# Retention stage of a two-layer hybrid attention block (fp32): rounds of one unit with decay on v, roots and affine products for two units at a time, and the gate in place

## What is computed

```python
log_gamma = jnp.log1p(-jnp.exp2(-5.0 - jnp.arange(h)))
decay = jnp.where(rel[None] >= 0, jnp.exp(jnp.maximum(rel, 0.0)[None] * log_gamma[:, None, None]), 0.0)
xi = jnp.exp((pos[:, None] + 1.0) * log_gamma[None, :])
zeta = jnp.exp((c - 1.0 - pos)[:, None] * log_gamma[None, :])
chunk_decay = jnp.exp(c * log_gamma)
inner = jnp.einsum('bnihd,bnjhd->bnhij', qc, kc) * decay
inner = jnp.einsum('bnhij,bnjhe->bnihe', inner, vc)
new_state = einsum('bjhd,bjhe->bhde', k_i * zeta, v_i) + chunk_decay * state
cross = jnp.einsum('bnihd,nbhde->bnihe', qc, prev_states) * xi
o = inner + cross
o = (o - mu) * lax.rsqrt(var + RET_GN_EPS)      # over the 64 columns of a head
return jax.nn.silu(g) * (o * gn_w + gn_b)
```

## Time and profile before

| | before |
|---|---|
| device time, median of 3 runs | 2778.09 us (2775.32 to 2784.47) |
| the profiled execution's own time | 2785.77 us |
| its span in the profile | 2784.0 us |
| granted TensorE clock, mean | 0.946 of 2.4 GHz |
| PE busy | 2620.7 us (94%) |
| DVE, ACT, POOL busy | 1537.3, 1105.9, 1036.0 us |
| retention stage of layer 0 (first transpose to first product of the output projection) | 558.0 to 653.0 us |
| the same of layer 1 | 1934.3 to 2029.3 us |

### The profile page before, as it was taken

The page is one execution under the profiler, slowest core; times in us unless marked ns, Lnnn a source line. Parts: engine busy times, 40 slices in busy tenths (PEclk is TensorE's granted clock), DMA queues, the critical chain, the costliest instruction groups (busy, mean ns, idle before and its releaser), DMA issues. The chain is left out here.

```text
span 2784.0 us, 43220 instructions
## 1 busy us (share of the span) xinstructions
PE 2620.7 (94%) x13164; PEld 2256.6 (81%) x13164; DVE 1537.3 (55%) x2969; ACT 1105.9 (40%) x2567; POOL 1036.0 (37%) x1229
## 2 busy tenths in 40 slices
PE   6999998989999999999989998988998999999997
PEld 5999877867778888888879998877777888888886
DVE  4666544373465445477656665433726544545785
ACT  4444543262532232244444445433515332323444
POOL 3455522183144544301044554221811555442012
PEclk9999999958999999999999999998599999999999
DMA  5111101121223332483331101012022323335633
GB/s 173 28 34 43 34 10 37 36 85 61 103 72 109 105 109 90 148 295 95 102 107 31 33 19 39 6 37 89 31 90 75 110 80 108 113 102 204 233 97 121
DMA packets 238653, 243.09 MB, mean 87 GB/s; under 512 B 27904, under 2 KB 170752, under 8 KB 238464
## 3 DMA queue, kind: packets, MB, share of 16 engines
q1 hardware_dynamic: 238464, 240.83, 26.9%
HBM read 173.14 MB, written 67.63 MB: 86 GB/s over the span
## 5 line engine op out<-in xcount | busy, mean ns | idle before, releaser
L2281 POOL TENSOR_TENSOR fw_a_lo<-fw_a_raw,fw_a_hi 128x512 fp32r<-128x512 f32 x132 | 179.9, 1363 | 524.1 <-DVE fw_s_raw L1875 524.1
L2281 POOL TENSOR_TENSOR fw_s_lo<-fw_s_raw,fw_s_hi 128x512 fp32r<-128x512 f32 x176 | 229.8, 1318 | 51.9 <-ACT fw_s_hi L1393 51.9
L702 PE MATMUL banks<-ht_hi,da_hi 128*128 128x512 f32 x496 | 192.9, 389 | 0.0
L702 PE MATMUL banks<-ht_lo,da_hi 128*128 128x512 f32 x496 | 192.9, 389 | 0.0
L702 PE MATMUL banks<-ht_hi,da_lo 128*128 128x512 f32 x496 | 192.9, 389 | 0.0
L702 PE MATMUL banks<-w_diff_hi,ht_hi 128*128 128x384 f32 x512 | 182.0, 355 | 6.2 <-DVE ht_lo L1579 4.1
L1206 ACT ACTIVATE pt_hi<-banks 128x512 fp32r<-128x512 f32 (+2 forms) x144 | 67.4, 502 | 291.1 <-PE banks L805 291.0
L702 PE MATMUL banks<-w_diff_hi,ht_lo 128*128 128x384 f32 x512 | 173.6, 339 | 0.0
L702 PE MATMUL banks<-w_diff_lo,ht_hi 128*128 128x384 f32 x512 | 173.5, 339 | 0.0
L2120 POOL TENSOR_TENSOR qk_rot<-rope_a,rope_b 128x512 f32<-128x512 f32 x64 | 82.7, 1292 | 213.5 <-DVE rope_b L1608 213.5
L1636 DVE TENSOR_REDUCE stats<-banks 128x1 f32<-128x1024 f32 (+3 forms) x192 | 138.6, 749 | 40.1 <-PE banks L903 35.3
(11 more groups left out here) (354 smaller groups left out, 7781.5 us busy)
## 6 DMA issues: line engine op xcount, KB each, us to landing
da_raw<-act_scratch SPq DMA_DIRECT2D x154, 256.0 KB, 2.7
fw_a_raw<-in_w_gate_dram SPq DMA_DIRECT2D x88, 256.0 KB, 3.1
act_scratch<-act_s SPq DMA_DIRECT2D x66, 256.0 KB, 2.9
w_diff_raw<-in_w_in_dram SPq DMA_DIRECT2D x24, 512.0 KB, 6.0
fw_a<-in_w_up_dram SPq DMA_DIRECT2D x44, 256.0 KB, 3.2
fw_a_raw<-in_w_up_dram SPq DMA_DIRECT2D x44, 256.0 KB, 2.9
act_scratch<-act_zero SPq DMA_DIRECT2D x44, 256.0 KB, 2.4
act_scratch<-act_one SPq DMA_DIRECT2D x44, 256.0 KB, 2.8
```

The source lines that it names most:

```text
L702: mm = pe.matmul(bank, lhsT, rhs, start=first and i == 0, stop=last and i == len(pairs) - 1, skip_group_check=resumes)
L2281: pool.tensor_tensor(w[1][:], w[2][:], w[0][:].bitcast(F32), ALU.subtract).then_inc(S["f_lo"], 1)
```

## The change

The decay between tokens i and j of a chunk, gamma^(i-j), is taken apart. v of token j is scaled by gamma^-(j+1)/8 (in place, on DVE, during latent attention), the score table becomes a plain causal 0/1 matrix, and the outer factor gamma^(i+1) is left out: the norm over a head's 64 columns cancels it, if the epsilon is divided by its square. So q and k need no scaled copies: `ret_scaled` is gone, PE transposes two blocks of a unit instead of three, and k is split unscaled. The state is multiplied by chunk_decay when it is split (ACT L1330 by its scale, DVE `ret_state_low` L1827 instead of POOL).

Roots are taken for two units in one call (four values). Normalizing moves from DVE to ACT (`ret_normed`, scale and bias, L1339), for which DVE computes the bias of two units (`ret_offset`, L1835). `ret_finish` multiplies and adds over two units in one instruction each. The gate's silu stays in r_z instead of r_gate.

The loops run over `RET_STEPS`, 24 rounds u. In round u each engine takes what others made in the round ahead. The quarters of the first output weights are split in rounds 4, 7, 10 and 13. `load_out(1)` waits for the finish of ten units (r_mx at 5 pairs), because r_z of units 0 to 9, in its place, now holds gates. The transposes of mixed_rows go in another order: the six columns of blocks that don't come from retention for both halves of the rows, then the last two for both.

```diff
-    rt_hi = [sb(f"rt_hi{i}", [P, 3, P], F32R, HT + 12 * KB + 1536 * i) for i in range(3)]
+    rt_hi = [sb(f"rt_hi{i}", [P, 2, P], F32R, HT + (12 + i) * KB) for i in range(3)]
...
+        RET_STEPS = range(RET_UNITS + 8)
+        ROUND_OUT = {4: 0, 7: 1, 10: 2, 13: 3}
# SP
-                arrives(decay[:], decay_dram.rearrange("p (a n) -> p a n", a=RET_PAIRS), "ret_in")
+                arrives(causal[:], causal_dram, "ret_in")
...
-                sp.wait_ge(S["r_xz"], L * PER["r_xz"] + T + 2)
-                sp.wait_ge(S["r_vlo"], L * PER["r_vlo"] + T + 2)
+                sp.wait_ge(S["r_mx"], L * PER["r_mx"] + T // 2 + 1)
                 sp.sem_inc(S["passed"], 1)
-                sp.wait_ge(S["tr_done"], L * PER["tr_done"] + RING - 2 * 2 * KD - RET_UNITS + T + 2)
                 load_out(1)
...
-                    sp.wait_ge(S["tr_done"], L * PER["tr_done"] + RING - NORM2_RINGS - 2 * KD + (half + 1) * KD)
+                    sp.wait_ge(S["tr_done"], L * PER["tr_done"] + RING - NORM2_RINGS - 2 + 2 * half)
# PE
-                    pe.wait_ge(S["r_xz"], L * PER["r_xz"] + n + 1)
+                    pe.wait_ge(S["rope_sum"], L * PER["rope_sum"] + ROPE_RET + n + 1)
...
-                    pe.transpose(bank[:, tokens(2)], r_xzt[n % 3][:, 0:2, :].rearrange("p a d -> p (a d)"), ident[:])\
-                        .then_inc(S["tr_done"], 1)
...
+                for u in RET_STEPS:
+                    if u < RET_UNITS:
+                        ret_transpose(u // T, u % T)
+                    if 0 <= u - 1 < RET_UNITS:
+                        ret_inner((u - 1) // T, (u - 1) % T)
+                    if 0 <= u - 2 < RET_UNITS:
+                        ret_output((u - 2) // T, (u - 2) % T)
...
-                transpose_rows(mixed_rows[:, 0:4, :], "r_mx", T + 4)
-                transpose_rows(mixed_rows[:, 4:8, :], "r_mx", 2 * T)
+                for blocks in (range(KD - 2), range(KD - 2, KD)):
+                    for half in range(2):
+                        if blocks[0]:
+                            pe.wait_ge(S["r_mx"], L * PER["r_mx"] + T // 2 + 2 * half + 2)
+                        transpose_rows(mixed_rows[:, 4 * half:4 * half + 4, :], "mix_in", 16, blocks)
# ACT
+                def ret_normed(n):
+                    m, i = n // 2, n % 2
+                    b = m % 2
+                    act.wait_ge(S["r_nb"], L * PER["r_nb"] + m + 1)
+                    if m >= 2:
+                        act.wait_ge(S["r_mx"], L * PER["r_mx"] + m - 1)
+                    for j in range(2):
+                        st = act.activation(r_norm[b][:, i, 64 * j:64 * j + 64], r_sum[m % 3][:, i, j, :], ACT.Identity,
+                                            bias=r_nb[:, b, 2 * i + j:2 * i + j + 1], scale=r_rs[:, b, 2 * i + j:2 * i + j + 1])
+                    st.then_inc(S["r_on"], 1)
...
+                for u in RET_STEPS:
+                    if u < RET_UNITS:
+                        ret_high(u)
+                        ret_high_k(u)
+                    if u + 2 < RET_UNITS:
+                        ret_gate_and_v(u + 2)
+                    if 0 <= u - 7 < RET_UNITS:
+                        ret_normed(u - 7)
+                    if 0 <= u - 1 < RET_UNITS:
+                        ret_inner(u - 1)
+                    if u in ROUND_OUT:
+                        weights(CH_OUT, [ROUND_OUT[u]])
                 weights(CH_OUT + 1)
# DVE
+                    v = r_z[n][:, 2 * P:3 * P].rearrange("p (j d) -> p j d", j=2)
+                    dve.tensor_tensor(v, v, xz[:, n // T, 0:2].unsqueeze(2).to_broadcast([P, 2, RET_DIM]), ALU.mult)
...
+                for u in RET_STEPS:
+                    if 0 <= u - 3 < RET_UNITS:
+                        ret_take(u - 3)
+                    if u < RET_UNITS:
+                        ret_low(u)
+                    if 0 <= u - 1 < RET_UNITS:
+                        ret_inner(u - 1)
+                    if 0 <= u - 3 < RET_UNITS:
+                        ret_moments(u - 3)
+                    if u >= 6 and u % 2 == 0 and u // 2 - 3 < RET_UNITS // 2:
+                        ret_offset(u // 2 - 3)
+                    if u + 2 < RET_UNITS:
+                        ret_low_v(u + 2)
+                    if 0 <= u - 1 < RET_UNITS:
+                        ret_state_low(u - 1)
# POOL
+                for u in RET_STEPS:
+                    if u < RET_UNITS:
+                        ret_low_k(u)
+                    if 0 <= u - 1 < RET_UNITS:
+                        ret_inner(u - 1)
+                    if u >= 5 and u % 2 == 1 and (u - 5) // 2 < RET_UNITS // 2:
+                        ret_root((u - 5) // 2)
+                    if u >= 9 and u % 2 == 1:
+                        ret_finish((u - 9) // 2)
+                    if u in ROUND_OUT:
+                        weights(CH_OUT, [ROUND_OUT[u]])
                 weights(CH_OUT + 1)
```

More of the change, by code:

```diff
@@ L1367, in _ @@
                         ret_gate_and_v(n)
[L1368 to L1380 removed]
+                for u in RET_STEPS:
[10 more added lines that the diff above has]
+                        weights(CH_OUT, [ROUND_OUT[u]])
                 weights(CH_OUT + 1)
[L1384 to L1385 removed]
+                for blocks in (range(KD - 2), range(KD - 2, KD)):
+                    for half in range(2):
+                        high_rows(half, None, blocks)
                 def gu_high(m, g, names):
@@ L1880, in h_low @@
                         .then_inc(S["h_lo"], 1)
-                for half in range(2):
-                    low_rows(half, None)
+                for blocks in (range(KD - 2), range(KD - 2, KD)):
+                    for half in range(2):
+                        low_rows(half, None, blocks)
                 for q in range(2 * T):
@@ L2248, in ret_root, with ret_finish @@
+                    pool.wait_ge(S["r_ms"], L * PER["r_ms"] + m + 1)
                     inverse_root(r_rs[:, b, :], r_ms[:, b, :]).then_inc(S["r_rstd"], 1)
-                def ret_finish(n):
-                    b, p = n % 2, n // T
-                    pool.wait_ge(S["r_on"], L * PER["r_on"] + n + 1)
+                def ret_finish(m):
+                    b, p = m % 2, 2 * m // T
+                    pool.wait_ge(S["r_on"], L * PER["r_on"] + 2 * m + 2)
                     cols = slice(p * P, (p + 1) * P)
-                    if n == 0:
+                    w, bias = (x[:, cols].unsqueeze(1).to_broadcast([P, 2, P]) for x in (gn_w, gn_b))
+                    if m == 0:
@@ L2263, in _ @@
[L2263 to L2273 removed]
+                    pool.tensor_tensor(r_norm[b][:], r_norm[b][:], w, ALU.mult).then_inc(S["r_gw"], 1)
@@ new lines, in ret_finish @@
+                    pool.wait_ge(S["r_gw"], L * PER["r_gw"] + m + 1)
+                    pool.tensor_tensor(r_norm[b][:], r_norm[b][:], bias, ALU.add).then_inc(S["r_gb"], 1)
+                    pool.wait_ge(S["r_gate"], L * PER["r_gate"] + 2 * m + 2)
+                    pool.wait_ge(S["r_gb"], L * PER["r_gb"] + m + 1)
+                    for i in range(2):
+                        n = 2 * m + i
+                        st = pool.tensor_tensor(mixed_rows[:, n % T, MIX_RET + p * P:MIX_RET + (p + 1) * P], r_norm[b][:, i, :],
+                                                r_z[n][:, 3 * P:4 * P], ALU.mult)
```

182 lines of the change are left out of this document (60 added, 122 removed).

## The result

| | before | after |
|---|---|---|
| device time, median of 20 runs each | 2778.91 us | 2786.60 us |
| ratio of after to before | | 1.0023, 95% interval 1.0017 to 1.0029 |
| the profiled execution's own time | 2785.77 us | 2787.85 us |
| its span | 2784.0 us | 2786.0 us |
| granted clock, mean | 0.946 | 0.946 |

Every engine has less to do, and the kernel is 0.23% slower. By the ratio the change is +6.4 us (0.0023 of 2779; the two medians differ by 7.7), which is under the 0.3% that the prediction called no change. The median, 2786.6, lies in the whole range of 2765 to 2796, but 0.2 above the bound of no change (2786.4, counted from the earlier median of before, 2778.09; that of the 20 runs is 2778.91) and 0.6 above the likeliest case's own range, 2774 to 2786.

A forecast was written before the change was run, and what follows sets the result against it. PE was taken to bound the later retention units, POOL those with a weight quarter, and ACT's and DVE's blocks the end. (0.0 + 1.2) × 2 layers = +2.4 us gave a median of 2780, whole range 2765 to 2796.

The forecast's parts named there:

- Rounds of 4.35: PE's retention rounds: without the third transpose, each falls by 0.22 us from 4.57 to 4.35.
- Start, taken 0: Start of retention, where DVE waits 3.2 us for gn_b: a saving of 0 to 1 us, taken as 0.
- PE ends about 629.1: End of PE's retention units: about 629.1 instead of 639.5, a gain of 10.4 us per layer inside the stage.
- POOL's pair: POOL's work in two rounds: root 1.4, finish 2.5, sum 6.1 us, 8.4 with a quarter, against PE's 8.7.
- SP asks at 630.9: Request for the second output weights: issued at 630.9 after the tenth unit's finish, landing at 638.70.
- The last finishes at 634.4, 636.9 and 639.4: POOL's pairs 5 to 7 at the stage's end: each 2.5 us, finished ahead of the banks.
- The gain is handed back, 0.0: Stage end: late weights in ACT's queue put the projection at 653.0 against 652.98, 0.0 us per layer; chance 0.62.
- The clock in the tail, 0 to +2.7, taken +1.2: Tail transposes of mixed_rows: up to twelve blocks at half clock, 0 to +2.7 us per layer, taken +1.2.
- Rival B, the full clock in the stage: Retention stage at 2.4 GHz: PE's round halves, POOL becomes the bound, about 2759 us; chance 0.07.
- Rival D, DVE and POOL hold each other up: Retention rounds: DVE's small SBUF instructions drawn out beside POOL's, DVE pacing the stage; 2793 us, chance 0.15.
- Rivals C and E: C: fifth finish three to five us earlier, about 2770, chance 0.10. E: tail at half clock, 2783 to 2788, chance 0.06.
- Scaling v costs nothing: Latent attention: DVE's 16 small products hidden under PE, taken 0, at most 9 us if DVE were the bound.

The follow-up runs named there:

- the repeat: The changed kernel run and traced once more, unchanged; 1.0022 of the kernel before, 2786.6 us.
- rows_first: Changed kernel with ACT's blocks of mixed_rows ahead of its copies of the second output weights; 0.9978 of the kernel before, 2774.9 us.
- before_rows_first: Kernel before with ACT's blocks of mixed_rows put ahead of its copies of the second output weights; ratio 0.9992.
- gates_own: Changed kernel with gates of units 0 to 9 in own tiles, so the second output weights are requested early; 1.0010 of the kernel before, 2782.6 us.
- before_dve2: Kernel before with two extra value-preserving DVE products per retention unit during latent attention, ACT's copy of v waiting for DVE; ratio 1.0017.
- no_vscale: Changed kernel without the scaling of v by the decay; 1.0008 of the kernel before.
- best3: Changed kernel with ACT's blocks reordered ahead of weights' copies, three normalized-pair tiles, weight quarters in rounds 1 to 4, v scaled on POOL; ratio 0.9929, 2758.3 us.
- early_quarters: Changed kernel with the four weight quarters in rounds 1 to 4 instead of 4, 7, 10 and 13; 1.0018 of the kernel before, 2783.8 us.

## Why the prediction was right, and where it was not

The path was right and the verdict was right by little: the forecast was +2.4 us and 2780, measured were +6.4 and 2786.6, at the very edge of what was called no change. Two costs that stood at nothing in the sum, the scaling of v and DVE held up by POOL, were not nothing, and a start that came earlier than forecast offset part of them. That the class came out is in part luck.

Of the steps, in the prediction's order, with times from the request for the table (558.3 in the kernel before, 557.2 in after):

- *Rounds of 4.35.* Measured 4.34 to 4.36 from unit 3 on. Two rounds are shorter, 3.7 and 2.97, by 2.0 us together where the prediction subtracted 1.8, and the one with the third quarter takes 4.43 to 4.50, or 6.7 as the long round.
- *Start, taken 0.* This term was off. Unit 3's first transpose stood at +10.3 before, and stands at +7.4 to +8.5 in the four layers of the changed kernel, 2 to 3 us earlier, though DVE's wait for gn_b is no shorter (3.1 to 4.0 us).
- *PE ends about 629.1*, which is +70.8. Measured 629.17, which is +71.9 with the long round; +68.9 and +69.7 in the repeat, +70.0 in layer 1. The ten us inside the stage were there, and a little more.
- *POOL's pair.* A root was put at 1.4 and a finish at 2.5; they take 1.26 (626.61 to 627.87) and 2.55. The row of the same width was the right one to lean on.
- *SP asks at 630.9*, +72.6. Measured +73.4, +71.5, +70.4 and +71.2. The transfer took 7.8, ACT's copies 3.90. That 630.66 came so near to 630.9 in the first trace is luck: the three layers without the long round are 1.1 to 2.2 ahead of the forecast.
- *The last finishes at 634.4, 636.9 and 639.4.* Measured 634.5, 637.0 and 639.5. But the prediction doesn't say what the first of them holds up: ACT's last normalizing waits 2.58 us for it, because there are only two tiles for normalized pairs, and so ends at 636.0.
- *The gain is handed back, 0.0.* Measured +0.4 us per layer on the mean of four layers, with the tail in it; -0.3 in the three without the long round. rows_first shows that the place is ACT's queue: 11.7 us come back by changing nothing but its order, and before_rows_first that the old order cost nothing before. gates_own splits the cause in two, 2.4 for the landing, 3.8 for the copies.
- *The clock in the tail, 0 to +2.7, taken +1.2.* In after the second transposes began at 0.50 and had 0.80 in the window from 648; 48 of them took 8.86 us against 7.23, +1.6. In layer 1 it was 8.24 against 7.24, in the repeat 8.90 and 8.39. The estimate holds. The slow blocks come from a clock that had fallen again: PE stood still from 632.8, the granted clock was 1.00 in 633 to 636 and 0.50 from 636. The Trainium skill's statement in "TensorE: Matmul & The Clock Gate", section "Part 4: PE-mode transpose", was that transposes don't raise the clock. Here too it rose in the middle of them, from 0.50 in 648 to 649 to 1.00 in 650 to 651 with nothing else on PE since 643.62, and the trace does not agree.
- *Rival B, the full clock in the stage*, did not come: 0.50 from 592 to 632. The Trainium skill's advice in "TensorE: Matmul & The Clock Gate", section "Why this matters for your kernels", is to keep TensorE busy without a gap for full throughput. After tests this less well than before did, since PE was busy 36.36 of these 40 us, with a wait of 2.11 in them.
- *Rival D, DVE and POOL hold each other up*, was half right in its mechanism and wrong in its size. They don't pace the rounds, but one instruction of DVE was held for a whole quarter of the weights, 2.2 us for PE, in four of twelve layers. That is 0.7 us per layer, about 1.5 of the 6.4.
- *Rivals C and E.* Not seen. The fifth finish came at most 2.2 us ahead of its forecast, not three to five, and the tail cost 1.0 to 1.7 us, not 2.7.
- *Scaling v costs nothing.* This step failed. I took 0 because PE paces latent attention, and did not look for the steps in which PE waits for DVE: the wait of 4.5 us for m_sum was in the trace of before. By before_dve2 one product per unit costs 2.4 us in all, if the cost goes with their number (its interval, halved, is 1.1 to 3.5); no_vscale and best3 point to 4 to 6.

The sum now: the stage +0.4 per layer (+0.7 with the two layers of no_vscale, 95.1 and 96.5, which run the same stage), 0.8 to 1.4 in all, and the scaling 2.4 to 5.7, together 3.2 to 7.1, against 6.4 measured (4.7 to 8.1 by its interval). The forecast of +2.4 had +1.2 per layer for the stage, which took +0.4 with the long rounds, and nothing for the scaling of v, which is what made it too small. Still open is where the rest of the scaling's price falls. The steps of latent attention that repeat show less than 1 us per layer for one product. The length of the whole latent attention differs by 2 us and more between executions, in jumps of some 1.5 us that come with and without the product: in before the first m_sum of a layer stands 27.3 us behind its first mq_lo (DVE's low part of a query) in layer 1 and 28.8 in layer 0, and at the same place of the two the granted clock was 0.73 (1737.2 to 1741.2) and 0.50 (358.7 to 362.7). Whether the scaling makes such jumps more frequent is not shown. That DVE is held by POOL is read from coincident rows; early_quarters took the quarter out of that round and the long round was gone in both layers, but no run had the two instructions by themselves.

## What to carry to other kernels

When a stage gets faster in the middle, follow its last transfer: a wait that is made later to reuse a buffer may be covered today only by the work that the change removes, and whatever stands behind it in an engine's order is then late too. Put work that the next stage needs at its start ahead of work that it needs halfway; here swapping two loops on one engine was worth 11.7 us. And an engine busy less than half the time (DVE 88.2 of the 211 us of latent attention) is not free at every step: extra instructions are hidden only where nobody waits for that engine, so look at its rows in the waits before costing them at nothing.

## What was not expected of the hardware

An instruction of DVE on 128x128 elements took 0.34 us or 2.52, depending on whether it started at least 0.03 or at most 0.02 us ahead of POOL's 128x1024 subtraction (eight layers and four). Such a coincidence makes identical layers of one program differ by 2 us. And the profiled executions of one kernel differed by up to 6.9 us in span (2786.0 and 2779.1) at mean clocks of 0.946 and 0.949.
